# One decoder layer on one core: VectorE reads the up half of the SwiGLU from PSUM itself

## The reference

```
h = rmsnorm(x, ffn_norm)
g = jnp.einsum('bsd,df->bsf', h, w_gate)
u = jnp.einsum('bsd,df->bsf', h, w_up)
x = x + jnp.einsum('bsf,fd->bsd', jax.nn.silu(g) * u, w_down)
```

## Time and profile before

| what | value |
|---|---|
| median of three runs | 294.89 us |
| the profiled execution | 295.2 us |
| its span, first to last instruction | 293.4 us |
| TensorE busy | 284.5 us, 97% |
| VectorE busy | 262.6 us, 89% |
| ScalarE busy | 190.5 us, 65% |
| GpSimd busy | 20.5 us, 7% |

### The profile page before, as it was taken

The page is one execution under the profiler, slowest core; times in us unless marked ns, Lnnn a source line. Parts: engine busy times, 40 slices in busy tenths (PEclk is TensorE's granted clock), DMA queues, the critical chain, the costliest instruction groups (busy, mean ns, idle before and its releaser), DMA issues.

```text
span 293.4 us, 4124 instructions
## 1 busy us (share of the span) xinstructions
PE 284.5 (97%) x1396; PEld 231.9 (79%) x1396; DVE 262.6 (89%) x422; ACT 190.5 (65%) x323; POOL 20.5 (7%) x30
## 2 busy tenths in 40 slices
PE   8999999999999999999999999999999999999990
PEld 4778878888888787888888878888888888888880
DVE  3888999999798999897598999999999999988984
ACT  4788567747696677766557665748484846664624
POOL 0001000000131420200000000000000000000063
PEclk9999999999999999999999999999999999999998
DMA  7999516797867966466847668695748382313003
GB/s 226 418 420 375 193 45 204 220 282 216 282 200 197 359 214 243 171 183 231 284 170 227 235 206 330 183 350 163 308 122 345 96 349 65 138 37 143 2 0 143
DMA packets 29653, 62.87 MB, mean 214 GB/s; under 512 B 3648, under 2 KB 16960, under 8 KB 28224
## 3 DMA queue, kind: packets, MB, share of 16 engines
q1 hardware_dynamic: 27616, 61.04, 60.7%
q10 hardware_dynamic: 2016, 1.57, 1.8%
HBM read 55.72 MB, written 1.11 MB: 194 GB/s over the span
## 4 chain that ended last, share of the span: by engine, by line
PE 57%; DVE 3%; issue 1%; POOL 1%; ACT 0%; POOLq 0%; ACTq 0%
PE bank L626 19%; PE bank L627 19%; PE bank L628 19%; DVE qkT_lo L1408 1%; DVE xs L1589 1%; POOL rot L1689 1%; DVE w_lo L1252 0%; POOLq L273 0%; PE bank L636 0%; DVE xs L1396 0%; DVE x_lo L1263 0%; ACT rot L1239 0%; DVE probs L1581 0%; DVE xs L1595 0%; DVE probs L1583 0%
## 5 line engine op out<-in xcount | busy, mean ns | idle before, releaser
L626 PE MATMUL bank<-w_hi,x_hi 128*128 128x512 f32 x224 | 88.9, 397 | 0.5 <-DVE w_lo L1252 0.5
L628 PE MATMUL bank<-w_hi,x_lo 128*128 128x512 f32 x224 | 87.3, 390 | 0.0
L627 PE MATMUL bank<-w_lo,x_hi 128*128 128x512 f32 x224 | 87.3, 390 | 0.0
L626 PEld LDWEIGHTS bank<-w_hi,x_hi 128*128 128x128 f32 x224 | 42.0, 188 | 11.4 <-DVE w_lo L1252 0.9
L628 PEld LDWEIGHTS bank<-w_hi,x_lo 128*128 128x128 f32 x224 | 42.0, 188 | 8.9
L627 PEld LDWEIGHTS bank<-w_lo,x_hi 128*128 128x128 f32 x224 | 42.1, 188 | 8.1
L940 ACT ACTIVATE w_hi<-raw 128x1024 fp32r<-128x1024 f32 x32 | 32.4, 1048 | 10.8 <-issue 9.6
L1252 DVE TENSOR_TENSOR w_lo<-raw,w_hi 128x1024 fp32r<-128x1024 f32 x32 | 38.3, 1211 | 0.8 <-ACT w_hi L940 0.7
L1408 DVE TENSOR_TENSOR w_lo<-raw,w_hi 128x1024 fp32r<-128x1024 f32 x30 | 36.0, 1215 | 0.4 <-ACT w_hi L1070 0.2
L1087 ACT ACTIVATE rope_b<-bank,rstd 128x256 f32<-128x256 f32 x22 | 10.4, 472 | 33.0 <-PE bank L628 32.7
L1070 ACT ACTIVATE w_hi<-raw 128x1024 fp32r<-128x1024 f32 x30 | 30.8, 1052 | 0.3 <-PE bank L628 0.3
(11 more groups left out here) (151 smaller groups left out, 477.6 us busy)
## 6 DMA issues: line engine op xcount, KB each, us to landing
raw<-in_weights SPq DMA_DIRECT2D x74, 512.0 KB, 5.7
room<-in_weights SPq DMA_DIRECT2D x10, 1024.0 KB, 7.0
room<-room SPq DMA_DIRECT2D x76, 64.0 KB, 2.2
room<-in_first SPq DMA_DIRECT2D x1, 1024.0 KB, 9.1
xs<-in_x SPq DMA_DIRECT2D x2, 512.0 KB, 9.5
rot<-turned_sums SPq DMA_DIRECT2D x8, 128.0 KB, 4.0
room<-in_first SPq DMA_DIRECT2D x2, 384.0 KB, 5.7
room<-room ACTq DMA_DIRECT2D x12, 64.0 KB, 2.7
```

The lines of the kernel that those rows point to most:

```text
L626: pe.matmul(dst, a_hi, w1, start=first, stop=False)
L627: pe.matmul(dst, a_hi, w2, start=False, stop=False)
L628: return pe.matmul(dst, a_lo, w1, start=False, stop=last)
```

## The change

ScalarE's second evacuating operation (L1088) goes, and with it the tensor `up`. VectorE's multiply becomes a scalar_tensor_tensor: (up half in PSUM x a scale per row) x silu. Since VectorE is now the last reader of the bank, TensorE's waits for `evacuated` become waits for `hid_ready`, which VectorE's multiply raises. `evacuated` is now raised by the activation alone. The numbers in the two semaphores run alike (one for each half of each chunk).

```
-        up = room[:, 3 * NB:4 * NB].rearrange("p (s f) -> p s f", s=SH)
...
                 if c == 0:
-                    pe.wait_ge(evacuated, 4)
+                    pe.wait_ge(hid_ready, 4)
...
                 pe.wait_ge(hid_ready, SH * NCH)
-                pe.wait_ge(evacuated, 2 * NCH)
...
-                pe.wait_ge(evacuated, 2 * c if c > 2 else 1)
+                pe.wait_ge(hid_ready, 2 * c if c > 2 else 1)
...
-                pe.wait_ge(evacuated, 2 * c + 1)
+                pe.wait_ge(hid_ready, 2 * c + 1)
...
-                act.activation(silu[:, s, :], src[:, 0:FC], ACT.Silu, scale=rstd[:, 6 + s:7 + s])
-                act.activation(up[:, s, :], src[:, FC:2 * FC], ACT.Copy,
-                               scale=rstd[:, 6 + s:7 + s]).then_inc(evacuated, 1)
+                act.activation(silu[:, s, :], src[:, 0:FC], ACT.Silu, scale=rstd[:, 6 + s:7 + s]).then_inc(evacuated, 1)
...
                 dve.wait_ge(evacuated, 2 * c + s + 1)
-                dve.tensor_tensor(hid[:, s, :], up[:, s, :], silu[:, s, :], ALU.mult).then_inc(hid_ready, 1)
+                dve.scalar_tensor_tensor(hid[:, s, :], gate_up_bank(c, s)[:, FC:2 * FC], rstd[:, 6 + s:7 + s],
+                                         silu[:, s, :], ALU.mult, ALU.mult).then_inc(hid_ready, 1)
```

## The result

The changed kernel takes 298.15 us (median of four runs, 298.08 to 298.74), the kernel before 294.90: ratio 1.0111, 95% interval 1.0098 to 1.0123, that is 2.9 to 3.6 us more. Forecast were 298.1 us and +3.2 us. The profiled execution took 298.17 us, its span is 296.4. All ratios are of executions in the fast state; two single ones in a slower state (304.7 us of experiment 7's kernel, 1018 us of the kernel before) are left out.

The account below looks back on a forecast made before the run. TensorE's waits were taken to bound the kernel. Two holds costing 1.74 us each, less an old loss of 0.27, gave +3.21 us: 298.1 us as a median, own range 297.6 to 298.6, wider range 297.0 to 299.4.

Parts of the forecast that it names:

- What bounds the kernel: TensorE, busy 97% of the span; work taken from ScalarE buys nothing, only a TensorE wait made or unmade moves the end.
- The price of the multiply: VectorE's new multiply reading PSUM takes 474 ns, bounds 421 to 540; the old one takes 421.
- Release of the bank: From the end of VectorE's multiply to TensorE's held load: 0.06 us, as for ScalarE's copy.
- Holds A and B: TensorE's loads before (3,0) (A) and (4,0) (B) wait for VectorE's multiply, 1.85 us each, each costing 1.74.
- Step 4: No hold in either half; the old loss of 0.27 us is gone; slack 0.44 us in the second half.
- Steps 5 to 10: No hold; slacks 0.36 to 0.38 us in steps 5 and 6, closest 0.20 us at (9,0).
- The sum: 1.74 + 1.74 - 0.27 = +3.21 us over the whole kernel, 298.1 us for a median.
- Only hold A: Rival, chance 0.08: hold before (3,0) lets VectorE catch up, so none before (4,0); +1.47 us, 296.4.
- More holds: Rival, chance 0.10: in steps 4 to 6 three more holds of 0.2 to 0.5 us; 298.7 to 299.6.
- The clock: Rival, chance 0.05: TensorE's clock falls in a hold, each losing 1.75 us more; 299.8 to 301.6.
- Not slower: Rival, chance 0.05: L1477 starts before TensorE's `down_first` ends, so both holds in steps 2 and 3 vanish; 294.6.

Follow-up runs that it names:

- experiment 7: Changed kernel with multiplies put ahead of work that can wait, on ScalarE's and VectorE's queues, steps 2 to 9: ratio 1.0187 to the kernel before.
- experiment 1: Kernel before with only TensorE's waits moved to VectorE's multiply; ScalarE's copy and the old multiply stay: ratio 1.0122.
- experiment 6: Kernel before with ScalarE's copy out of the bank widened from 256 to 512 columns, 22 times: ratio 1.0007.
- experiment 5: Changed kernel with the second half's multiply put ahead of the sums of down weights on VectorE's queue, in step 2 alone: ratio 1.0051 to the kernel before.
- experiment 2: New form from chunk 4 on; chunks 0 to 3 keep the copy, old multiply and old waits: ratio 1.0032 to the kernel before.
- experiment 4: Changed kernel with the second half's multiply put ahead of the sums of down weights on VectorE's queue, in steps 2 and 3: ratio 1.0047 to the kernel before.
- experiment 3: New form from chunk 6 on only; earlier chunks keep the copy, old multiply and old waits: ratio 0.9998 to the kernel before.
- experiment 12: Kernel before with VectorE's queue reordered in steps 2 to 6: multiplies and transpose ahead of sums, first half's multiply also ahead of one split: ratio 1.0024.

## Why the prediction was right

**What bounds the kernel.** Right: only TensorE's waits mattered. 7.4 us less on ScalarE and 1.0 more on VectorE show nowhere in the time but through them: experiment 1 has neither and the same two holds, and experiment 6 has 4.4 us more on ScalarE and one hold 0.2 us longer.

**The price of the multiply.** Taken as 474 ns by the nearest row. The changed kernel's group of it:

```profile
L1415 DVE SCALAR_TENSOR_TENSOR rope_a<-bank,rstd,rope_b 128x256 f32<-128x256 f32 x22 | 10.5, 479 | 3.2 <-ACT rope_b L1085 3.2
```

479 ns, 5 over. By the figure of the Trainium skill (Perfetto Trace Analysis, Optimizing Scalar/DVE Operations) it would, as an estimate, have been 65 ns over its like in SBUF. The page gives that figure for engine-busy time and calls the profiled latency about twice as much. The rows show neither: L1268, the SBUF form, is at 481 in the same trace.

**Release of the bank.** 151.22 + 0.48 = 151.70, load at 151.75: 0.05, forecast 0.06.

**Holds A and B.** Forecast 1.85 each, measured 1.85 and 1.84 by spacing. By the matmul two behind the held load each cost 1.74 and 1.73, as worked out; the 0.03 us that follows was not in the working. The step that could most easily have failed, that hold A gives VectorE no time to catch up, holds: the distance of 8.3 us stayed, and experiment 5 shows B without A.

**Step 4.** The hold of 0.38 before (4,1) is gone, as forecast, since TensorE came later, not since the copy is gone. Experiments 2 and 4 show it: with TensorE on time there, the new multiply holds it 1.3 to 1.4 us. The slack behind the multiply of (4,1) was forecast as 0.44 us with the release of 0.06 already taken off; in the trace it is 0.44 with the release still in it, so 0.06 less.

**Steps 5 to 10.** No hold, as forecast. In steps 5 and 6 the multiplies end 0.49 to 0.52 us ahead, release taken off, where 0.36 to 0.38 was forecast. In step 9 the reason given was too good: VectorE was said to be tied to TensorE there, with 0.20 us to spare, and with TensorE less late the new multiply holds it by 0.12 and 0.20 us (experiments 3 and 4). That nothing was held there in the changed kernel seems to owe something to the two holds ahead of it.

**The sum.** +3.21 forecast, 3.27 in the trace of the steps, 3.25 between the medians. The 0.06 us between the first two is twice the 0.03 us behind each hold.

**The rivals.** *Only hold A*: out, there are two. *More holds*: none. *The clock*: the changed kernel in the stretch with both holds (columns as in the earlier trace rows):

```profile
140.00:170.00 30.00, 27.07 (x119) 21.77 (x118) 24.18 (x34) 16.66 (x21) 0.00 (x0) 1.00 0.62 219
```

The granted clock is 1.00, 2.4 GHz, through both. So the rule of the Trainium skill that idle gaps can throttle the clock (TensorE: Matmul & The Clock Gate, HAM oscillation) did not come into play for these gaps, 1.5 us without a matmul and 1.85 without a weight load. *Not slower*: L1122 still waited for TensorE, 2.30 and 1.89 us.

## What to carry to other kernels

When a change moves the last read of a buffer to another engine, what counts is not the price of the read but where that engine's queue stands at that moment: compare, at every reuse, the end of the new last reader with the time at which the waiting engine wants the buffer. Busy shares hid the whole cost here, since ScalarE at 65% was prompt and VectorE at 89% was not. A copy that looks like waste can be what keeps a late engine from holding another (experiment 12). Where the late engine is itself released by the one it holds, a hold does not heal the next one; and an order that gains at one place must be followed to the end of the queue, since what stood ahead of the moved step is now late.

## What the runs showed of the hardware that was not expected

- A 128x256 scalar_tensor_tensor takes VectorE as long with an operand in PSUM (479 ns) as from SBUF (481).
- TensorE went without work for some 1.5 us twice and kept its full clock; matmuls 128x512 were 0.23 us apart from the second one on.
- A hold of a weight load costs TensorE 0.11 to 0.12 us less than its length at the second matmul behind it (0.38 cost 0.27, 1.86 cost 1.74). Loads in the unheld stream start 0.22 to 0.23 us ahead of their matmuls. The next ten matmuls, at 0.230 us and not 0.227, cost another 0.03 us.
